# Five levels of a gated linear attention: products of 64 keys with the 32 right-half queries in place of 32 by 32

## What is computed

```
def _chunk_gated_recurrence(q, k, v, logf):          # per head, state S of 128 x 128
    # S_t = diag(f_t) S_{t-1} + k_t v_t^T ; o_t = S_t^T q_t
    ...
        b = jnp.cumsum(gc, axis=2)
        diff = b[:, :, :, None, :] - b[:, :, None, :, :]
        decay = jnp.exp(jnp.minimum(diff, 0.0)) * tri[:, :, None]
        A = jnp.einsum('bhtsd,bhsd->bhts', qc[:, :, :, None, :] * decay, kc)
        o = (jnp.einsum('bhts,bhsv->bhtv', A, vc) + ...
```

## Time and profile before

| | |
|---|---|
| median of three runs | 995.21 us |
| the profiled execution's own time | 997.04 us |
| its span, first to last instruction | 995.2 us |
| TensorE busy | 983.3 us (99%), 8050 matmuls |
| VectorE busy | 672.6 us (68%) |
| ScalarE busy | 593.6 us (60%) |
| GpSimd busy | 25.4 us (3%) |
| mean granted TensorE clock | 0.996 of full speed |
| mean rate of the DMAs | 167 GB/s |

### The profile page before, as it was taken

The page is one execution under the profiler, slowest core; times in us unless marked ns, Lnnn a source line. Parts: engine busy times, 40 slices in busy tenths (PEclk is TensorE's granted clock), DMA queues, the critical chain, the costliest instruction groups (busy, mean ns, idle before and its releaser), DMA issues.

```text
span 995.2 us, 18822 instructions
## 1 busy us (share of the span) xinstructions
PE 983.3 (99%) x8050; PEld 890.0 (89%) x8050; DVE 672.6 (68%) x896; ACT 593.6 (60%) x829; POOL 25.4 (3%) x26
## 2 busy tenths in 40 slices
PE   8999999999999999999999999999999999999996
PEld 7899987888989999998899999889899999987985
DVE  5675688867755788875556565785695556588565
ACT  7677576574537656654446676537754765654581
POOL 0000000000000000000000003000000000130000
PEclk9999999999999999999999999999999999999999
DMA  8762434656565665557654553553556446534331
GB/s 297 270 200 92 150 115 161 210 170 205 176 193 191 187 192 171 170 169 253 190 156 148 147 173 115 163 158 129 172 168 193 151 118 190 170 129 142 137 128 42
DMA packets 97283, 166.45 MB, mean 167 GB/s; under 512 B 6896, under 2 KB 32240, under 8 KB 96816
## 3 DMA queue, kind: packets, MB, share of 16 engines
q1 hardware_dynamic: 95792, 159.18, 50.7%
q0 software_dynamic: 976, 4.46, 1.3%
q10 hardware_dynamic: 432, 1.62, 0.4%
HBM read 164.19 MB, written 1.05 MB: 166 GB/s over the span
## 4 chain that ended last, share of the span: by engine, by line
PE 94%; DVE 2%; ACT 2%; issue 1%; DMA 1%; SPq 0%; DVEq 0%; ACTq 0%
PE proj L623 14%; PE proj L624 14%; PE proj L625 14%; PE proj L632 13%; PE proj L634 13%; PE proj L633 13%; PE mix L668 1%; PE mix L944 1%; PE mix L693 1%; PE mix L676 1%; PE mix L905 1%; PE mix L893 1%; DMA raw<-in_w_mem_kv 1%; ACT arena L1372 1%; PE mix L701 1%
## 5 line engine op out<-in xcount | busy, mean ns | idle before, releaser
L1532 DVE TENSOR_TENSOR wlo<-raw,whi 128x1024 fp32r<-128x1024 f32 (+2 forms) x304 | 356.6, 1202 | 177.3 <-ACT whi L1067 176.0
L1067 ACT ACTIVATE whi<-raw 128x1024 fp32r<-128x1024 f32 (+2 forms) x304 | 307.3, 1040 | 185.4 <-PE proj L634 81.3
L623 PE MATMUL proj<-act_hi,whi 128*128 128x256 f32 x1064 | 304.0, 286 | 0.5 <-ACT arena L1345 0.5
L624 PE MATMUL proj<-act_lo,whi 128*128 128x256 f32 x1064 | 301.0, 283 | 0.0
L625 PE MATMUL proj<-act_hi,wlo 128*128 128x256 f32 x1064 | 301.0, 283 | 0.0
L623 PEld LDWEIGHTS proj<-act_hi,whi 128*128 128x128 f32 x1064 | 203.2, 191 | 3.0 <-ACT arena L1345 1.4
L624 PEld LDWEIGHTS proj<-act_lo,whi 128*128 128x128 f32 x1064 | 203.3, 191 | 0.5
L625 PEld LDWEIGHTS proj<-act_hi,wlo 128*128 128x128 f32 x1064 | 203.2, 191 | 0.2
L632 PE MATMUL proj<-whi,y_hi 128*128 128x512 f32 (+1 forms) x340 | 133.3, 392 | 1.3 <-DVE wlo L1532 1.3
L634 PE MATMUL proj<-whi,y_lo 128*128 128x512 f32 (+1 forms) x340 | 132.3, 389 | 0.0
L633 PE MATMUL proj<-wlo,y_hi 128*128 128x512 f32 (+1 forms) x340 | 132.3, 389 | 0.0
(11 more groups left out here) (335 smaller groups left out, 1027.4 us busy)
## 6 DMA issues: line engine op xcount, KB each, us to landing
raw<-in_w_in SPq DMA_DIRECT2D x144, 512.0 KB, 4.4
raw<-in_w_up SPq DMA_DIRECT2D x88, 256.0 KB, 4.4
raw<-in_w_out SPq DMA_DIRECT2D x32, 512.0 KB, 3.5
raw<-in_w_down SPq DMA_DIRECT2D x22, 512.0 KB, 5.7
raw<-in_w_mem_k SPq DMA_DIRECT2D x8, 512.0 KB, 4.0
raw<-in_w_o SPq DMA_DIRECT2D x8, 512.0 KB, 3.9
raw<-in_w_mem_v SPq DMA_DIRECT2D x8, 512.0 KB, 4.1
raw<-in_w_mem_kv SPq DMA_DIRECT2D x7, 512.0 KB, 6.7
```

The source lines that it names most:

```text
L623: mm(o, wh[:, i, wc], hi[:, k0 + i, :], start=begin and j % 2 == 0, stop=False, skip_group_check=True)
L624: mm(o, wh[:, i, wc], lo[:, k0 + i, :], start=False, stop=False, skip_group_check=True)
L1067: fn(whi[c % SPLIT][:, 0:w], raw[c % SLOTS][:, 0:w], ACT.Copy).then_inc(s.w_hi, 1)
L1532: tt(wlo[c % SPLIT][:, 0:w], raw[c % SLOTS][:, 0:w], f32(whi[c % SPLIT][:, 0:w]), ALU.subtract).then_inc(s.w_lo, 1)
```

## The change

- Levels 7 to 3 become 32 products (8 heads, 2 blocks, 2 groups n of 64 tokens): 64 keys by the 32 queries that stand in right halves, which are read with a stride from `HQP`. Output partitions 64n to 64n+64, columns 64h + 32b as before. Level 8 stays 64 products of 32 by 32.
- `AC` has 16 blocks of 64 query columns, 1024 in all, where it had 16 of 32. `masked(l)` writes the 32 right-half columns of each block, in runs of h; level 8 writes all 64, reading its 32 columns twice, and so clears what is off the diagonal. The masks are 64 tokens wide; the constants grow by 32 columns.
- `leave_32()` copies level 2 into `AC` instead of `AT`, and `diagonal()` comes behind it (and behind the split `hgg1`, 0), in two copies of 64 partitions by 1024 columns.
- GpSimd clears 4096 columns instead of 3584, since `AC` is larger. The gate totals of the halves 4 to 64 move to a part of `under_y` that is free then.

```
-    node = lambda h: (i % 32 // (2 * h) == np.arange(32)[None, :] // (2 * h))
-    masks = [node(h) & (i % (2 * h) < h) & (np.arange(32)[None, :] % (2 * h) >= h) for h in SMALL]
-    masks.append(i % 32 == np.arange(32)[None, :])
+    right = lambda h: np.array([t for t in range(64) if t % (2 * h) >= h])[None, :]
+    masks = [(i % 64 // (2 * h) == right(h) // (2 * h)) & (i % (2 * h) < h) for h in SMALL]
+    masks.append(i % 64 == np.arange(64)[None, :])
...
-        total = sb("total", [P, 2016])
+        total = sb("total", [P, 1024])
...
-        AT, AC = ar(0, HG_H, TRI), ar(3072, 16, 32)
+        AT, AC = ar(0, HG_H, TRI), ar(3072, 16, 64)
...
-                nc.gpsimd.memset(arena[:, 0:3584], 0.0).then_inc(s.hg_zero, 1)
+                nc.gpsimd.memset(arena[:, 0:4096], 0.0).then_inc(s.hg_zero, 1)
...
                             zk, zq = HKT[:, h, :], (HQT if l == 8 else HQP)[:, h, :]
-                            if l >= 3:
+                            if l == 8:
                                 for b in range(NB):
                                     for j in range(4):
                                         t, at_col = slice(b * P + 32 * j, b * P + 32 * j + 32), 64 * h + 32 * b
                                         last = mm(mix[32 * j:32 * j + 32, LEVEL_BANK[l], at_col:at_col + 32], zk[:, t], zq[:, t], start=True, stop=True)
+                            elif l >= 3:
+                                for b in range(NB):
+                                    for n in range(2):
+                                        t, at_col = slice(b * P + 64 * n, b * P + 64 * n + 64), 64 * h + 32 * b
+                                        right = zq[:, t].rearrange("p (n s t) -> p n s t", s=2, t=SMALL[l - 3])[:, :, 1, :]
+                                        last = mm(mix[64 * n:64 * n + 64, LEVEL_BANK[l], at_col:at_col + 32], zk[:, t], right, start=True, stop=True)
...
                 def diagonal():
 
                     act.wait_ge(s.hg_cp, 6 * L + 6)
-                    for j in range(4):
-                        rows = slice(32 * j, 32 * j + 32)
-                        last = fn(both(AT[rows, :, 32 * j:32 * j + 32], HG_H, 32), AC[rows, :, :].rearrange("p (h b) t -> p h b t", b=2), ACT.Copy)
+                    act.wait_ge(s.hg_ca, 6 * L + 2)
+                    for n in range(2):
+                        rows = slice(64 * n, 64 * n + 64)
+                        last = fn(both(AT[rows, :, 64 * n:64 * n + 64], HG_H, 64), AC[rows, :, :].rearrange("p (h b) t -> p h b t", b=2), ACT.Copy)
                     last.then_inc(s.hg_at, 1)
 
                 def leave_32():
 
-                    act.wait_ge(s.hg_zero, L + 1)
+                    act.wait_ge(s.hg_cp, 6 * L + 6)
                     act.wait_ge(s.hg_pr, 18 * L + 14)
...
-                        fn(both(AT[rows, :, 64 * n + 32:64 * n + 64], HG_H, 32), src, ACT.Copy).then_inc(s.hg_ca, 1)
+                        fn(AC[rows, :, 32:64].rearrange("p (h b) t -> p h b t", b=NB), src, ACT.Copy).then_inc(s.hg_ca, 1)
...
-                diagonal()
                 split_until(ahead_of("hgg1", L, 0))
                 leave_32()
+                diagonal()
...
-                    nc.vector.copy_predicated(AC, over(level[:, l - 3, :], 16), src).then_inc(s.hg_cp, 1)
+                    if l == 8:
+                        out, mask = AC.rearrange("p n (s t) -> p n s t", s=2), level[:, 160:224].rearrange("p (s t) -> p s t", s=2)
+                        src = src.unsqueeze(2).to_broadcast([P, 16, 2, 32])
+                    else:
+                        half = SMALL[l - 3]
+                        out = AC.rearrange("p n (m s t) -> p n m s t", s=2, t=half)[:, :, :, 1, :]
+                        mask = level[:, 32 * (l - 3):32 * (l - 2)].rearrange("p (m t) -> p m t", t=half)
+                        src = src.rearrange("p n (m t) -> p n m t", t=half)
+                    nc.vector.copy_predicated(out, over(mask, 16), src).then_inc(s.hg_cp, 1)
```

More of the change, by code:

```diff
@@ L54, in constants @@
         "hide": np.concatenate([np.where(i >= j, 0, NEG), none, np.where(i >= j, 0, NEG)], 1),
-        "level": np.stack(masks, 1).astype(np.float32).reshape(P, -1),
+        "level": np.concatenate(masks, 1).astype(np.float32),
         "inv": np.broadcast_to(inv.astype(np.float32), (P, ROPE // 2)),
@@ L397, in stack_kernel @@
         pick = cst("pick").rearrange("p (h m) -> p h m", h=ML_H)
-        level = cst("level").bitcast(U32).rearrange("p (l t) -> p l t", t=32)
+        level = cst("level").bitcast(U32)
         def ar(at, *dims):
@@ L498, in stack_kernel @@
         FORGET = const[:, CONST_AT["tri"][0]:CONST_AT["pick"][1]].rearrange("p (h t) -> p h t", t=SEQ)
-        AT, AC = ar(0, HG_H, TRI), ar(3072, 16, 32)
+        AT, AC = ar(0, HG_H, TRI), ar(3072, 16, 64)
         HKT, HQP = under_y[:, 0, 0:8, :], under_y[:, 1, 0:8, :]
-        TOTAL = {1: FORGET.rearrange("p h t -> p (h t)"), 2: total[:, 0:1024], 4: total[:, 1024:1536], 8: total[:, 1536:1792],
-                 16: total[:, 1792:1920], 32: total[:, 1920:1984], 64: total[:, 1984:2016]}
+        SPARE = [under_y[:, n, 12:14, :].rearrange("p k t -> p (k t)") for n in range(2)]
+        TOTAL = {1: FORGET.rearrange("p h t -> p (h t)"), 2: total[:, :], 4: SPARE[0], 8: SPARE[1][:, 0:256],
+                 16: SPARE[1][:, 256:384], 32: SPARE[1][:, 384:448], 64: SPARE[1][:, 448:480]}
         HQT, HSQ, HV, HGT = ar(14336, 8, SEQ), ar(10240, 8, SEQ), ar(12288, NB, DM), ar(8192, 8, SEQ)
```

## The result

The changed kernel takes 1000.43 us (median of six runs, 999.41 to 1002.39) against 995.0 (994.36 to 996.04) for the kernel before: ratio 1.0055, interval 1.0042 to 1.0068, so 4.2 to 6.8 us slower. I had forecast 1000.3, with 997.0 to 1002.5 as range. The span of the profiled execution went from 995.2 to 999.2, where I had forecast 1000.3.

The account below looks back on a forecast made before the run. TensorE, busy for 99% of the span, was taken to bound the kernel. Longer levels add 2.76 us in layer 0 and 2.36 in layer 1, so 995.21 + 5.1 = 1000.3 us, range 997.0 to 1002.5.

Parts of the forecast that it names:

- The pace of a level: TensorE, levels 7 to 3: 64-column loads set each strip's pace, 58 ns a pair, 2.00 us a level against 1.29.
- The strided queries at zero: Levels 7 to 3: reading the moving operand with a stride costs zero; up to 0.9 us a level was thought possible.
- The stalls inside two levels counted as gone: Level 3 of layer 0 and level 4 of layer 1: stalls of 0.26 and 0.62 us disappear; 0.9 more if they stay.
- Levels 7 and 6 with 0.61 of cover, 0.81 a layer: Ahead of L913: these levels grow 1.42 us together, 0.61 hidden by its wait for VectorE, 0.81 a layer left.
- The copies of levels 7 and 6 at zero: VectorE's copies with shorter runs, still 512 columns, cost zero; bounded by 0.4 us for level 6.
- The level 8 copy: VectorE: 512 to 1024 columns, at most 0.75 us more, covered by 0.86 of idle ahead of L1908.
- ScalarE and GpSimd at zero: Diagonal copies, at most 2.5 us and done by 680, and the memset, 3.1 to 3.5 us, cost zero.
- The first one: Levels 7 to 3: the longer load hides, 1.13 us a level, 1.7 us faster, 993.5; chance 10%.
- The second: Levels 7 to 3: TensorE pays by the matmul, 0.65 us a level, 4.6 us faster, 990.6; chance 4%.
- The third: Levels 7 to 3: strips don't load side by side (3.7 us a level, 1017) or slow strided operand (1009); chance 5%.
- The sum: TensorE's path, levels 7 to 3: 2.76 us more in layer 0 and 2.36 in layer 1, 5.1 us in all.

Follow-up runs that it names:

- e3: Changed kernel with only the first 32 keys of each 64 as stationary operand in levels 7 to 3; 996.5 us, one run.
- e6: Changed kernel with only the first 48 keys of each 64 as stationary operand in levels 7 to 3; 996.68 us, one run.
- e2: Changed kernel with the first 32 queries of each 64, side by side, in place of the strided right halves in levels 7 to 3; 1001.61 us, one run.
- e1: Changed kernel with levels 7 to 3 back at 64 products of 32 by 32 on four strips, the rest kept; 996.16 us, ratio 1.0006 to the kernel before.
- e9: Kernel before, with VectorE's second softmax shares moved ahead of the level 6 copy and the growth of half 2; ratio 0.9989 to the kernel before.
- e5: Changed kernel with all 64 queries, side by side, as moving operand in levels 7 to 3; 1000.26 us, one run.
- e10: Kernel of e1 with the copies of levels 7 and 6 written in runs of 4 columns instead of 1 and 2; 994.65 us, one run.
- e11: Kernel of e1 with VectorE's second softmax shares moved ahead of the level 6 copy, as in e9; ratio 0.999 to the kernel before.

## Why the prediction was right, point by point

- **The pace of a level: right.** 2.00 foretold, 1.98 to 1.99 measured; loads of one strip 58 ns apart foretold, 58 to 59 measured; and e3 to e6 show that it goes with the load's columns and not with the queries. The step that carried it was to read a load's occupancy from two durations (109 and 136 ns) and not from what a matmul costs, and to look for a place where the load is longer than its matmul (L781). The second half carried more: 109 ns is the duration on four strips, and on two, at level 2, a load of 32 columns lasts 113, which would have given 0.72 a column. L781's 112 ns for 128 columns is the row that spoke for 0.84.
- **The strided queries at zero: right.** e2 shows it beside a load of 64 columns, where I had allowed that half speed would pass unseen; e3 and e1 show it beside loads of 32, where it would not.
- **The stalls inside two levels counted as gone: right**, in all ten new levels. But they are not a property of the kernel: the same TensorE program has them in level 3 of the first and level 4 of the second layer in the kernel before, and in e9 once, 0.48 us in level 3 of the first layer. In the changed kernel a smaller one, 0.14, sits in level 8 of the second layer, which kept its 128 matmuls. The sum took them from one execution, and which levels had them there is chance. The reason that I gave, that they are waits for instructions, no run shows; the rows say only "issue". (The second stall is 0.66 over 1.25 and not 0.62; the sum, which takes 1.91, is not touched.)
- **Levels 7 and 6 with 0.61 of cover, 0.81 a layer: right in size, incomplete in its reason.** Level 5 starts 0.81 later after level 8 than before (650.32 - 626.68 = 23.64 against 650.36 - 627.53 = 22.83); in the second layer it is 0.94, of which 0.14 is the stall in level 8. I said that TensorE itself would then be last ahead of the transposition. But the loads there still wait for VectorE (waits in the changed kernel, as in the earlier trace rows, which reads 1.8):

```profile
PEld mix L914 <- DVE arena L1925: 0.7, 2, 0.3
```

 The transposition starts 0.07 later than the projection would let it. The two chains nearly tie, because of the next point.
- **The copies of levels 7 and 6 at zero: wrong.** They last 0.59 longer each. I had bounded the second by 0.4, which was what VectorE would have in hand and so a cover, not a price; no row spoke for it. The longer level 6 delayed this copy besides, by the 0.3 that I had foretold. With 32 by 32 products, as in e1, this copy makes the transposition late by 0.6 a layer; in the changed kernel only the 0.07 is left of it, since TensorE's own 0.71 for each of the two levels hides the rest. That the mistake did not show in the time is luck.
- **The level 8 copy: right.** 1.38 us for 1024 columns, 0.63 more; L1916 still waits for TensorE, 0.22 in place of 0.86.
- **ScalarE and GpSimd at zero: right.** ScalarE in time, from level 2's copy to level 0's:

```profile
678.02 1.18 ACT L1408 ACTIVATE arena<-mix 32x512 f32<-32x512 f32 x2
679.30 2.13 ACT L1398 ACTIVATE arena<-arena 64x1024 f32<-64x1024 f32 x2
...
686.66 1.06 ACT L1422 ACTIVATE arena<-mix 128x512 f32<-128x512 f32 x2
```

 The diagonal takes 2.1 us instead of 2.5 and ends at 681.4 (I had said 680), the level 0 copies at 687.7; the products that need them start at 692.5 and wait for nobody. GpSimd's memset takes 3.5 us instead of 3.1, and nobody waits for it.
- **The rivals** at 10, 4 and 5% all fell. The first one's 1.13 needs loads of 32 columns (e3: 1.14); with 64 the load does not hide. The second falls with e1 against the changed kernel: 128 matmuls in 1.25 us, 64 in 1.99. The Trainium skill (TensorE: Matmul & The Clock Gate, Back-to-back issue gap) names a floor of about 25 ns between matmuls; across four strips they start 10 ns apart here. The third needed levels of 3.7 or 2.9 us.
- **The sum.** 2.76 and 2.36 a layer foretold, 2.71 and 2.16 in the trace. The second layer is 0.2 short because the kernel before lost about 0.2 among the matmuls of the values (L701, L702) and 0.08 in level 2 there and the changed one did not, which outweighs the changed one's 0.14 in level 8. That the forecast 1000.3 lies only 0.1 from the median of 1000.43 is luck too: the traces have 4.9 us, the medians differ by 5.4, and the interval is 2.6 us wide.

## What to carry to other kernels

Before merging small products into fewer larger ones, count what is loaded on each strip of the array: the pair costs the longer of load and matmul (plus 4 to 5 ns here), and halving the number of matmuls while the load doubles and the strips halve gains nothing and here loses 0.7 us a level (1.99 against 1.29). If the load must be 64 columns long, the moving operand may be 64 as well, for 0.02 us a level (e5). When an engine waits inside a tuned order, look first at what stands ahead of the awaited work on the other engine that nobody needs yet: one move of three instructions (e9) gave 1.1 us here.

## What was not expected of the hardware

A masked copy on VectorE of 512 fp32 columns takes 1.32 us when it writes runs of 1 or 2 columns with gaps of the same length, and 0.70 to 0.74 in runs of 4 or more (e10 puts the same two copies in runs of 4). The source and the mask are read alike in both. VectorE's product for the growth of half 1 reads and writes with a step of two as well, 1024 columns in 1.2 us like its contiguous ones, and isn't slowed; what differs was not tried. And TensorE's short stalls while it issues 128 matmuls of 10 ns move from place to place between executions, with up to 0.8 us from one matmul to the next (e1); none was seen inside the 50 levels of 64 matmuls that cost 1.97 to 2.02 us in six kernels, while level 2, whose 64 matmuls are 18 ns apart, still showed up to 0.36 (e11). The 20 levels of e3 and e6, with 64 matmuls 18 and 24 ns apart, had none. What causes them stays open.
